# A two-block transformer step on one Trainium2 core: the expert choice with its one-hot product and sum on GpSimd

## The chip, the cores and the metric

The program runs on one core of a Trainium2 chip. The metric is device time in microseconds (us), median of several runs. The engines named below are TensorE (PE in the rows, its weight loads PEld), VectorE (DVE), ScalarE (ACT), GpSimd (POOL) and SyncE (SP), which issues the weight stream.

## What is computed

256 tokens of width 1024 pass through two decoder blocks (retention, dilated attention, two feed-forward parts) and then through two further layers. Each of those ends in a product-key expert stage, which is where the change lies (8 heads, two sides of 128 scores each, `TOPK` = 16):

```python
def peer(xn, wq, k1, k2, u_tab, v_tab):
    q = (xt @ wq).reshape(t, PEER_HEADS, D_KEY)
    q1, q2 = q[..., :D_HALF], q[..., D_HALF:]
    s1 = jnp.einsum("thd,hnd->thn", q1, k1)
    s2 = jnp.einsum("thd,hnd->thn", q2, k2)
    v1, i1 = lax.top_k(s1, TOPK)
    v2, i2 = lax.top_k(s2, TOPK)
    cand = (v1[..., :, None] + v2[..., None, :]).reshape(t, PEER_HEADS, TOPK * TOPK)
    sv, ci = lax.top_k(cand, TOPK)
    e1 = jnp.take_along_axis(i1, ci // TOPK, axis=-1)
    e2 = jnp.take_along_axis(i2, ci % TOPK, axis=-1)
    gates = jax.nn.softmax(sv, axis=-1)
    ...
        hid = jax.nn.gelu(jnp.einsum("td,tkd->tk", xi, u_tab[ei]))
        return jnp.einsum("tk,tkd->td", gi * hid, v_tab[ei])
```

The kernel computes `hid` for all 16384 experts as a dense product and weights it with gates that are zero for the experts not chosen. So the choice of `e1`, `e2` and the gates has to be ready only when that weighting begins.

## The kernel before

All weights come through one stream of tiles of 128 x 1024 floats (512 KB), 878 in all. Each tile goes through the same steps. SyncE loads it into one of four `raw` buffers. ScalarE rounds it to the high half `wh` (`hi`, line 397), into one of two buffers, once TensorE has finished the tile two before (`mm_done`). VectorE writes the low half `wl = raw - wh` (`lo`, line 863) once `w_hi` says that `wh` is there. TensorE waits in `tile_a` (line 1545) for `w_lo` and for the evacuation of its PSUM bank, and then issues 24 matmuls, three passes for each of 8 blocks (lines 1534 to 1536). ScalarE evacuates the result (line 411). So every tile needs one `hi` and one `lo`, in that order, between the end of the tile two before and its own start.

In a layer `k` (0 or 1) of the second pair, 16 tiles give the queries, and 128 more give `hid`. `key_scores` (line 2006) multiplies queries with keys on TensorE, 16 matmuls for two heads, four times per layer, and ScalarE copies the scores to `sc` (line 760).

The expert choice runs on VectorE meanwhile, in 8 rounds `i` per layer (lines 1388 to 1462), each for two heads of one half of the tokens, with 128 tokens on the partitions. Its steps are written between the `lo` calls by hand: `tile()` waits for all the steps so far (`so_far`) and then issues one `lo`, so a round holds exactly 8 of them, and a `lo` is late when the steps ahead of it take long. The steps of a round: copy the scores to `cur` (line 1410); the eight largest of each of four rows of 128 (`max`, 1413), their indices (1416), the row with those struck out (`match_replace`, 1419), the next eight (1422); the 16 x 16 sums `cand` (1425); the indices of the next eight (1428) and their conversion to float `tf` (1430); the same top 16 over two rows of 256 (1432 to 1442); the scores less the largest (`ge`, 1444); the two 4-bit ranks out of each index (1448, 1449) and their conversion (1451). Then for each side `s`: `rank_hot`, a one-hot of the ranks over 16 places, 128x512 in `mh` (1398), and `onto_keys`, its product with the keys `tf` (1404) and the sum over the 16 places (1406) into `ee`. Every counted step raises `pick_step`; 43 of them make a round.

GpSimd issues DMAs alone (lines 330 to 376). In the loop over `k` it loads `bd` and the keys, and goes on to a wait near the end of the kernel.

After the 8 rounds the remaining `lo` follow one another. ScalarE takes the exponentials of `ge` at tile `U_PICK` = 56 of `hid` (line 777), TensorE transposes `ee` and `ge` after tile 59 (line 2034), and the gates are applied from tile 64 on.

Of the kernel before, what the change touches and what calls it, by code (L numbers as in the profile page):

```python
# [20 lines left out]
F32 = mybir.dt.float32  # L21
F32R = mybir.dt.float32r
U32 = mybir.dt.uint32
# [4 lines left out]
P = 128  # L28
# [19 lines left out]
NK, TOPK = 128, 16  # L48
EPS2 = 1e-6
RG_C = 8.0  # L50
PICK_STEPS = 43
MASKED = -1e30
LOWEST = -3.0e38

# [39 lines left out]
def build(nc, stream, x_in, consts, ret_c, att_c, vecs, rg_w, keys, scratch, out):  # L94
    with ExitStack() as ctx:
# [3 lines left out]
        def sem(name):  # L99
            return ctx.enter_context(nc.semaphore(name))  # L100
# [88 lines left out]
        def pick_part(off, *shape):  # L189
# [3 lines left out]
                                                   **dict(zip("abcd", shape)))  # L193


        cur, best = pick_part(1152, 2, 2, P), pick_part(1664, 2, 2, P)
        cand, cand2 = pick_part(1152, 2, 16, 16), pick_part(1664, 2, 256)
        hot = mh[:, 0:2, :].rearrange("p h (a b) -> p h a b", a=16)
        hot_out, hot = hot, hot.bitcast(F32)
        ee, ge = pick_part(0, 2, NC_T * H2, 16), pick_part(512, NC_T * H2, 16)  # L200
        tv, tf, ti = pick_part(768, 2, 2, 16), pick_part(832, 2, 2, 16), pick_part(896, 2, 2, 16).bitcast(U32)
        sv, ci = pick_part(960, 2, 16), pick_part(992, 2, 16).bitcast(U32)
        cr, crf = pick_part(1024, 2, 2, 16).bitcast(U32), pick_part(1088, 2, 2, 16)
        gd = pick_part(2176, 2, NC_T * H2)
        e1T, e2T, gT = (pickT[:, m, :] for m in range(3))

# [37 lines left out]
        k_in, p_s, p_sc, pick_step, p_exp, p_e, p_t, p_tc = (  # L244
            sem(s) for s in "keys_in peer_scores peer_scores_copied peer_pick_step peer_exp "
            "peer_picked peer_turned peer_turned_copied".split())
        g_hot, g_gated = sem("peer_onehots"), sem("peer_gated_rows")
        g_mm, g_mul = sem("peer_gates"), sem("peer_weighted")
        g_put, g_late = sem("peer_gates_put"), sem("peer_late_weighted")
# [79 lines left out]
        @block.gpsimd  # L329
        def _(pool):  # L330
            pool.dma_start(cst[:, :], consts).then_inc(const_in, 16)
            pool.dma_start(vec[:, :], vecs).then_inc(const_in, 16)
            pool.dma_start(xr[:, :, :], x_in.rearrange("(c p) d -> p c d", p=P)).then_inc(x_in_s, 16)
            pool.wait_ge(x_turned, 1)
            pool.dma_start(rc, ret_c).then_inc(retc_in, 16)

            def gains(k):

                pool.dma_start(ln_rows, bass.AP(norm_rows.tensor, 8 * k * P, [[0, P], [32 * P, 2], [1, D]])) \
                    .then_inc(ln_in, 16)  # L340

            pool.wait_ge(rows_copied, 1)
            pool.dma_start(norm_rows, vec_rows[0:104, :]).then_inc(rows_stored, 16)
            pool.wait_ge(rows_stored, 16)
            gains(0)
            pool.wait_ge(n_up, 2)
            gains(1)

            pool.wait_ge(n_lo, split_before[1])
            pool.dma_start(ac[0:33, :], att_c).then_inc(attc_in, 16)  # L350
            pool.wait_ge(b_vecc, G3)
            pool.dma_start(scratch.rearrange("g h x -> h g x"), bv[0:AH, :, :]).then_inc(b_store, 16)
            pool.wait_ge(b_store, 16)
            pool.wait_ge(n_up, 4)
            for h in range(AH):
                if h >= 4:
                    pool.wait_ge(a_b, h - 3)
                pool.dma_start(bs[:, h % 4, :, :], bass.AP(
                    scratch.tensor, h * 384, [[1, P], [AH * 384, G3], [1, T]])).then_inc(b_in[h % 4], 16)

            pool.wait_ge(n_up, 4)
            pool.wait_ge(a_b, AH)
            gains(2)
            pool.wait_ge(n_up, 6)
            gains(3)
            for k in range(2):
                pool.wait_ge(n_lo, split_before[5 + 2 * k])
                pool.dma_start(bd, rg_w[k]).then_inc(bd_in, 16)
                pool.wait_ge(n_lo, split_before[6 + 2 * k])
                pool.dma_start(pk, keys[k]).then_inc(k_in, 16)  # L370
            pool.wait_ge(m_lo, PAIR["b1"] + 10)
            pool.dma_start(ln_rows[:, 0, :], bass.AP(norm_rows.tensor, V_FIN * P, [[0, P], [1, D]])).then_inc(ln_in, 16)
            for c in range(NC_T):
                pool.wait_ge(o_ready, c + 1)
                pool.dma_start(out[c * P:(c + 1) * P, :], o_rows[:, c, :]).then_inc(o_stored, 16)
            pool.wait_ge(o_stored, 32)
# [470 lines left out]
        def _(dve):  # L847
# [364 lines left out]
            for k in range(2):  # L1212
# [175 lines left out]
                for i in range(8):  # L1388
                    pick[0] = 0
                    n = 8 * (i % 2) + 2 * (i // 2)  # L1390

                    def tile():
                        so_far(i)
                        lo(g0 + 29 + at[0] + 2)
                        at[0] += 1

                    def rank_hot(s):
                        count(V.tensor_tensor(hot_out, crf[:, s, :, :].unsqueeze(3).to_broadcast(B4),  # L1398
                                              iota16.unsqueeze(1).unsqueeze(1).to_broadcast(B4), ALU.is_equal))
                        so_far(i)  # L1400

                    def onto_keys(s):

                        count(V.tensor_tensor(hot_out, hot, tf[:, :, s, :].unsqueeze(2).to_broadcast(B4), ALU.mult))  # L1404
                        so_far(i)
                        count(V.tensor_reduce(ee[:, s, n:n + 2, :], hot, AX, ALU.add))  # L1406


                    dve.wait_ge(p_sc, 8 * k + i + 1)
                    count(V.tensor_copy(cur, sc[:, n:n + 2, :, :]))  # L1410
                    tile()
                    for a, s in sides:
                        count(V.max(tv[:, a, s, 0:8], cur[:, a, s, :]))
                    so_far(i)
                    for a, s in sides:
                        count(V.max_index(ti[:, a, s, 0:8], tv[:, a, s, 0:8], cur[:, a, s, :]))
                    tile()
                    for a, s in sides:
                        count(V.match_replace(best[:, a, s, :], tv[:, a, s, 0:8], cur[:, a, s, :], LOWEST))
                    so_far(i)  # L1420
                    for a, s in sides:
                        count(V.max(tv[:, a, s, 8:16], best[:, a, s, :]))

                    tile()
                    count(V.tensor_tensor(cand, tv[:, :, 0, :].unsqueeze(3).to_broadcast(B4),
                                          tv[:, :, 1, :].unsqueeze(2).to_broadcast(B4), ALU.add))
                    for a, s in sides:
                        count(V.max_index(ti[:, a, s, 8:16], tv[:, a, s, 8:16], best[:, a, s, :]))  # L1428
                    so_far(i)
                    count(V.tensor_copy(tf, ti))  # L1430
                    for a in range(2):
                        count(V.max(sv[:, a, 0:8], flat[:, a, :]))
                    tile()
                    for a in range(2):
                        count(V.max_index(ci[:, a, 0:8], sv[:, a, 0:8], flat[:, a, :]))
                        count(V.match_replace(cand2[:, a, :], sv[:, a, 0:8], flat[:, a, :], LOWEST))
                    so_far(i)
                    for a in range(2):
                        count(V.max(sv[:, a, 8:16], cand2[:, a, :]))
                    tile()  # L1440
                    for a in range(2):
                        count(V.max_index(ci[:, a, 8:16], sv[:, a, 8:16], cand2[:, a, :]))

                    count(V.tensor_tensor(ge[:, n:n + 2, :], sv, sv[:, :, 0:1].to_broadcast([P, 2, 16]),
                                          ALU.subtract))

                    tile()
                    count(V.tensor_single_scalar(cr[:, 0, :, :], ci, 4, ALU.logical_shift_right))
                    count(V.tensor_single_scalar(cr[:, 1, :, :], ci, 15, ALU.bitwise_and))
                    so_far(i)  # L1450
                    count(V.tensor_copy(crf, cr))
                    so_far(i)
                    rank_hot(0)
                    so_far(i)
                    onto_keys(0)
                    tile()
                    rank_hot(1)
                    onto_keys(1)
                    so_far(i)
                    assert pick[0] == PICK_STEPS  # L1460
                    lo(g0 + 29 + at[0] + 2)
                    at[0] += 1
# [65 lines left out]
        def _(pe):  # L1528
# [359 lines left out]
            for k in range(2):  # L1888
# [140 lines left out]
                    tile_a(g0 + 45 + j, e0 + 33 + j)  # L2029

                pe.wait_ge(p_e, k + 1)
                for c in range(NC_T):
                    for m, src in enumerate((ee[:, 0, :, :], ee[:, 1, :, :], ge)):
                        ins = nc.tensor.transpose(ps_x[:, c, m * P:(m + 1) * P],
# [170 lines left out]
```

## Time and profile before

| | us |
|---|---|
| median of 3 runs | 2948.59 |
| lowest, highest | 2946.07, 2948.68 |
| the profiled execution | 2945.24 |
| its span, first to last instruction | 2943.5 |
| TensorE busy | 2817.1 (96%) |
| VectorE busy | 1941.7 (66%) |
| ScalarE busy | 1557.4 (53%) |
| GpSimd busy | 23.0 (1%) |
| layer 0: 64 `lo` of the 8 rounds | 1101.1 to 1308.9 |
| layer 1: first and last copy of the scores | 2094.8 to 2276.9 |
| mean granted clock of TensorE | 0.989 |

Busy times of TensorE overlap, since matmuls are pipelined. A start time is therefore a better measure than a duration: steps are read below as the distance from one start to the next on the same engine.

### The profile page before, as it was taken

Reading aid. Unit: us, or ns where it says so; the run is one execution under the profiler, and the core shown is the slowest. Engines: PE = TensorE matmul, PEld = TensorE weight load, DVE = VectorE, ACT = ScalarE, POOL = GpSimd, SP = SyncE. Lnnn points to the kernel's source line nnn. Section 1 sums busy time; section 2 is a strip of 40 time slices with the busy share of each in tenths; the row PEclk is TensorE's granted clock in tenths of the full one; section 3 lists DMA queues with packets and bytes.
Section 4 is the critical chain, followed back from the end, with each engine's and each line's share of the span. In section 5 each row is a group of like instructions: output and inputs, shape, how many; then the busy total and the mean of one; then the engine's idle time right before and its main releaser. Section 6 shows DMA issues by size and latency. Waiting matters only on the chain.

```text
span 2943.5 us, 51574 instructions
## 1 busy us (share of the span) xinstructions
PE 2817.1 (96%) x18787; PEld 2548.3 (87%) x18787; DVE 1941.7 (66%) x3107; ACT 1557.4 (53%) x2815; POOL 23.0 (1%) x38
## 2 busy tenths in 40 slices
PE   8999999999999989999999999998999999999998
PEld 6988987898898879999998888887999999978886
DVE  5656454555555869986886555568799678855555
ACT  4455453555545564446775444456544577644444
POOL 0000000000000000000000000000000000000000
PEclk9999999999999999999999999999999999999999
DMA  6435556664554444454444555543444444455554
GB/s 219 151 130 183 185 170 180 172 159 149 165 184 159 133 130 164 158 170 143 138 144 144 192 190 189 191 161 109 163 161 163 159 140 143 138 178 192 190 189 149
DMA packets 158659, 480.26 MB, mean 163 GB/s; under 512 B 14608, under 2 KB 51472, under 8 KB 158128
## 3 DMA queue, kind: packets, MB, share of 16 engines
q1 hardware_dynamic: 154080, 460.38, 47.4%
q0 software_dynamic: 4432, 17.87, 2.6%
q8 instruction: 98, 1.61, 0.2%
q14 instruction: 49, 0.40, 0.0%
HBM read 477.02 MB, written 1.18 MB: 162 GB/s over the span
## 4 chain that ended last, share of the span: by engine, by line
PE 77%; DVE 16%; ACT 4%; issue 2%; DMA 1%; POOL 0%; DVEq 0%; ACTq 0%; POOLq 0%
PE ps L1534 23%; PE ps L1536 23%; PE ps L1535 23%; DVE wl L863 6%; PE ps L2049 4%; ACT wh L397 2%; DVE arena L1251 1%; DVE mh L1404 1%; DVE picks L1406 1%; DVE mh L1398 1%; PE ps L1653 1%; DMA raw<-stream_dram 1%; DVE xr L882 0%; PE ps L2015 0%; DVE picks L1428 0%
## 5 line engine op out<-in xcount | busy, mean ns | idle before, releaser
L863 DVE TENSOR_TENSOR wl<-raw,wh 128x1024 fp32r<-128x1024 f32 x878 | 1075.5, 1225 | 889.6 <-ACT wh L397 883.6
L397 ACT ACTIVATE wh<-raw 128x1024 fp32r<-128x1024 f32 x878 | 929.9, 1059 | 1281.8 <-PE ps L1536 1270.9
L1534 PE MATMUL ps<-xh,wh 128*128 128x256 f32 x3920 | 1138.9, 291 | 24.4 <-DVE wl L863 22.9
L1535 PE MATMUL ps<-xl,wh 128*128 128x256 f32 x3920 | 1111.5, 284 | 0.0
L1536 PE MATMUL ps<-xh,wl 128*128 128x256 f32 x3920 | 1110.9, 283 | 0.0
L1534 PEld LDWEIGHTS ps<-xh,wh 128*128 128x128 f32 x3920 | 753.4, 192 | 49.2 <-issue 36.9
L1535 PEld LDWEIGHTS ps<-xl,wh 128*128 128x128 f32 x3920 | 754.6, 193 | 0.4
L1536 PEld LDWEIGHTS ps<-xh,wl 128*128 128x128 f32 x3920 | 753.7, 192 | 0.0
L1534 PE MATMUL ps<-wh,mh 128*128 128x512 f32 x1304 | 516.6, 396 | 13.7 <-DVE ml L875 8.8
L1536 PE MATMUL ps<-wh,ml 128*128 128x512 f32 x1304 | 512.1, 393 | 0.0
L1535 PE MATMUL ps<-wl,mh 128*128 128x512 f32 x1304 | 511.0, 392 | 0.0
L1534 PEld LDWEIGHTS ps<-wh,mh 128*128 128x128 f32 x1304 | 246.0, 189 | 90.9 <-issue 33.3
L1536 PEld LDWEIGHTS ps<-wh,ml 128*128 128x128 f32 x1304 | 246.0, 189 | 54.2
L1535 PEld LDWEIGHTS ps<-wl,mh 128*128 128x128 f32 x1304 | 246.7, 189 | 43.5
L411 ACT ACTIVATE arena<-ps 128x256 f32<-128x256 f32 (+1 forms) x360 | 132.2, 367 | 0.2
L1534 PE MATMUL ps<-wh,xh 128*128 128x512 f32 x248 | 101.4, 409 | 15.5 <-DVE wl L863 5.7
L875 DVE TENSOR_TENSOR ml<-arena,mh 128x512 fp32r<-128x512 f32 x158 | 108.1, 686 | 4.4 <-ACT mh L443 4.4
L443 ACT ACTIVATE mh<-arena 128x512 fp32r (+1 forms) x158 | 96.9, 615 | 7.1 <-DVE arena L1494 3.9
L1494 DVE TENSOR_TENSOR arena<-arena,ps 128x260 f32<-128x260 f32 (+42 forms) x128 | 71.1, 556 | 42.7 <-ACT arena L817 40.9
L1535 PE MATMUL ps<-wl,xh 128*128 128x512 f32 x248 | 98.8, 398 | 0.0
L1536 PE MATMUL ps<-wh,xl 128*128 128x512 f32 x248 | 98.4, 397 | 0.0
L797 ACT ACTIVATE picks<-mh,pickT 128x128 f32<-128x128 f32 x256 | 81.5, 398 | 4.4 <-DVE mh L1482 4.4
(280 smaller groups left out, 2040.1 us busy)
## 6 DMA issues: line engine op xcount, KB each, us to landing
raw<-stream_dram SPq DMA_DIRECT2D x878, 512.0 KB, 3.3
arena<-bias_scratch POOLq DMA_DIRECT2D x16, 384.0 KB, 9.8
arena<-norm_rows POOLq DMA_DIRECT2D x4, 1024.0 KB, 6.8
arena<-keys_dram POOLq DMA_DIRECT2D x2, 1024.0 KB, 5.1
arena<-ret_c_dram POOLq DMA_DIRECT2D x1, 1344.0 KB, 6.1
xr<-x_dram POOLq DMA_DIRECT2D x1, 1024.0 KB, 9.2
out_dram<-arena POOLq DMA_DIRECT2D x2, 512.0 KB, 2.9
arena<-rg_w_dram POOLq DMA_DIRECT2D x2, 256.0 KB, 2.9
```

The costliest lines, as they stand in the source:

```text
L397: A(wh[b % 2][:, :, :], raw[:, b % 4, :].rearrange("p (a b) -> p a b", a=DB), ACT.Copy) \
L411: A(dst, src, func, scale=scale, **kw).then_inc(evac, 1)
L443: A(mh[:, s:s + 2, :], src, ACT.Copy).then_inc(m_hi, 1)
L797: ins = A(gated[n % 3][:, j, :], oh[n % 2][:, j, :].bitcast(F32), ACT.Copy, scale=gT[:, t:t + 1])
L863: V.tensor_tensor(wl[b % 2][:, :, :], raw[:, b % 4, :].rearrange("p (a b) -> p a b", a=DB), wh[b % 2][:, :, :].bitcast(F32), ALU.subtract) ...
L875: V.tensor_tensor(ml[:, s:s + 2, :], src, mh[:, s:s + 2, :].bitcast(F32), ALU.subtract) \
L1251: ins = V.scalar_tensor_tensor(out=cy[:, b, :], in0=src, scalar=vec[:, w:w + 1], in1=cy[:, b, :], op0=ALU.mult, op1=ALU.add)
L1494: V.tensor_tensor(h, h, ps_a[:, n % 4, :].rearrange("p (t m) -> p m t", t=4)[:, 0:known, :], ALU.mult).then_inc(g_mul, 1)
L1534: M(out_ap, lh, rh, start=first, stop=False, skip_group_check=skip)
L1535: M(out_ap, lh, rl, start=False, stop=False, skip_group_check=skip)
L1536: return M(out_ap, ll, rh, start=False, stop=last, skip_group_check=skip)
L2049: ins = M(ps_a[:, n % 4, j * P:(j + 1) * P], gated[n % 3][:, j, :], oh[n % 2][:, 4 + j, :].bitcast(F32), start=True, stop=True)
```

## The change

The copy of the scores is left out; `cur` is a view of `sc`. VectorE keeps everything up to the two one-hots. Those go to two buffers (`mh` for side 0, `ml` for side 1), each raises a semaphore `p_rank`, and GpSimd does the rest: the product with the keys, and the sum over 16 places as four additions that halve the number of places (8, 4, 2, then the last into `ee`), five instructions for a side, ten for a round, each waiting for the one before. `tf` has two buffers, in `pickT`. VectorE waits for GpSimd's `p_ee` ahead of a one-hot (round before, same side) and ahead of `tf` (two rounds before); TensorE waits for it ahead of the transposes. The steps are also dealt out anew between the 8 `lo` of a round, and `PICK_STEPS` is 36.

```diff
--- before.py
+++ after.py
@@ -48,7 +48,7 @@
 NK, TOPK = 128, 16
 EPS2 = 1e-6
 RG_C = 8.0
-PICK_STEPS = 43
+PICK_STEPS = 36
 MASKED = -1e30
 LOWEST = -3.0e38
 
@@ -193,14 +193,16 @@
                                                    **dict(zip("abcd", shape)))
 
 
-        cur, best = pick_part(1152, 2, 2, P), pick_part(1664, 2, 2, P)
+        best = pick_part(1664, 2, 2, P)
         cand, cand2 = pick_part(1152, 2, 16, 16), pick_part(1664, 2, 256)
-        hot = mh[:, 0:2, :].rearrange("p h (a b) -> p h a b", a=16)
-        hot_out, hot = hot, hot.bitcast(F32)
+        hot_out = [t[:, 0:2, :].rearrange("p h (a b) -> p h a b", a=16) for t in (mh, ml)]
+        hot = [t.bitcast(F32) for t in hot_out]
+        tf = [pickT[:, 0, 64 * n:64 * n + 64].rearrange("p (a b c) -> p a b c", a=2, b=2) for n in range(2)]
+        crf = pickT[:, 0, 128:192].rearrange("p (a b c) -> p a b c", a=2, b=2)
         ee, ge = pick_part(0, 2, NC_T * H2, 16), pick_part(512, NC_T * H2, 16)
-        tv, tf, ti = pick_part(768, 2, 2, 16), pick_part(832, 2, 2, 16), pick_part(896, 2, 2, 16).bitcast(U32)
+        tv, ti = pick_part(768, 2, 2, 16), pick_part(896, 2, 2, 16).bitcast(U32)
         sv, ci = pick_part(960, 2, 16), pick_part(992, 2, 16).bitcast(U32)
-        cr, crf = pick_part(1024, 2, 2, 16).bitcast(U32), pick_part(1088, 2, 2, 16)
+        cr = pick_part(1024, 2, 2, 16).bitcast(U32)
         gd = pick_part(2176, 2, NC_T * H2)
         e1T, e2T, gT = (pickT[:, m, :] for m in range(3))
 
@@ -244,6 +246,7 @@
         k_in, p_s, p_sc, pick_step, p_exp, p_e, p_t, p_tc = (
             sem(s) for s in "keys_in peer_scores peer_scores_copied peer_pick_step peer_exp "
             "peer_picked peer_turned peer_turned_copied".split())
+        p_rank, p_hot, p_ee = sem("peer_ranks"), sem("peer_keys_at_ranks"), sem("peer_keys_summed")
         g_hot, g_gated = sem("peer_onehots"), sem("peer_gated_rows")
         g_mm, g_mul = sem("peer_gates"), sem("peer_weighted")
         g_put, g_late = sem("peer_gates_put"), sem("peer_late_weighted")
@@ -368,6 +371,21 @@
                 pool.dma_start(bd, rg_w[k]).then_inc(bd_in, 16)
                 pool.wait_ge(n_lo, split_before[6 + 2 * k])
                 pool.dma_start(pk, keys[k]).then_inc(k_in, 16)
+                B4 = [P, 2, 16, 16]
+                for i in range(8):
+                    n = 8 * (i % 2) + 2 * (i // 2)
+                    for s in range(2):
+                        done = 2 * (8 * k + i) + s
+                        pool.wait_ge(p_rank, done + 1)
+                        nc.gpsimd.tensor_tensor(hot_out[s], hot[s], tf[i % 2][:, :, s, :].unsqueeze(2).to_broadcast(B4),
+                                                ALU.mult).then_inc(p_hot, 1)
+                        for step, w in enumerate((8, 4, 2)):
+                            pool.wait_ge(p_hot, 4 * done + step + 1)
+                            nc.gpsimd.tensor_tensor(hot_out[s][:, :, :, 0:w], hot[s][:, :, :, 0:w],
+                                                    hot[s][:, :, :, w:2 * w], ALU.add).then_inc(p_hot, 1)
+                        pool.wait_ge(p_hot, 4 * done + 4)
+                        nc.gpsimd.tensor_tensor(ee[:, s, n:n + 2, :].unsqueeze(3), hot[s][:, :, :, 0:1],
+                                                hot[s][:, :, :, 1:2], ALU.add).then_inc(p_ee, 1)
             pool.wait_ge(m_lo, PAIR["b1"] + 10)
             pool.dma_start(ln_rows[:, 0, :], bass.AP(norm_rows.tensor, V_FIN * P, [[0, P], [1, D]])).then_inc(ln_in, 16)
             for c in range(NC_T):
@@ -1394,45 +1412,37 @@
                         lo(g0 + 29 + at[0] + 2)
                         at[0] += 1
 
-                    def rank_hot(s):
-                        count(V.tensor_tensor(hot_out, crf[:, s, :, :].unsqueeze(3).to_broadcast(B4),
-                                              iota16.unsqueeze(1).unsqueeze(1).to_broadcast(B4), ALU.is_equal))
-                        so_far(i)
-
-                    def onto_keys(s):
-
-                        count(V.tensor_tensor(hot_out, hot, tf[:, :, s, :].unsqueeze(2).to_broadcast(B4), ALU.mult))
-                        so_far(i)
-                        count(V.tensor_reduce(ee[:, s, n:n + 2, :], hot, AX, ALU.add))
-
-
                     dve.wait_ge(p_sc, 8 * k + i + 1)
-                    count(V.tensor_copy(cur, sc[:, n:n + 2, :, :]))
-                    tile()
+                    cur = sc[:, n:n + 2, :, :]
                     for a, s in sides:
                         count(V.max(tv[:, a, s, 0:8], cur[:, a, s, :]))
-                    so_far(i)
+                    tile()
                     for a, s in sides:
                         count(V.max_index(ti[:, a, s, 0:8], tv[:, a, s, 0:8], cur[:, a, s, :]))
                     tile()
                     for a, s in sides:
                         count(V.match_replace(best[:, a, s, :], tv[:, a, s, 0:8], cur[:, a, s, :], LOWEST))
-                    so_far(i)
+                    tile()
                     for a, s in sides:
                         count(V.max(tv[:, a, s, 8:16], best[:, a, s, :]))
-
-                    tile()
+                    so_far(i)
                     count(V.tensor_tensor(cand, tv[:, :, 0, :].unsqueeze(3).to_broadcast(B4),
                                           tv[:, :, 1, :].unsqueeze(2).to_broadcast(B4), ALU.add))
+                    tile()
                     for a, s in sides:
                         count(V.max_index(ti[:, a, s, 8:16], tv[:, a, s, 8:16], best[:, a, s, :]))
                     so_far(i)
-                    count(V.tensor_copy(tf, ti))
+                    if 8 * k + i >= 2:
+                        dve.wait_ge(p_ee, 2 * (8 * k + i - 1))
+                    count(V.tensor_copy(tf[i % 2], ti))
+                    tile()
                     for a in range(2):
                         count(V.max(sv[:, a, 0:8], flat[:, a, :]))
+                    so_far(i)
+                    for a in range(2):
+                        count(V.max_index(ci[:, a, 0:8], sv[:, a, 0:8], flat[:, a, :]))
                     tile()
                     for a in range(2):
-                        count(V.max_index(ci[:, a, 0:8], sv[:, a, 0:8], flat[:, a, :]))
                         count(V.match_replace(cand2[:, a, :], sv[:, a, 0:8], flat[:, a, :], LOWEST))
                     so_far(i)
                     for a in range(2):
@@ -1440,23 +1450,21 @@
                     tile()
                     for a in range(2):
                         count(V.max_index(ci[:, a, 8:16], sv[:, a, 8:16], cand2[:, a, :]))
-
                     count(V.tensor_tensor(ge[:, n:n + 2, :], sv, sv[:, :, 0:1].to_broadcast([P, 2, 16]),
                                           ALU.subtract))
-
-                    tile()
+                    so_far(i)
                     count(V.tensor_single_scalar(cr[:, 0, :, :], ci, 4, ALU.logical_shift_right))
                     count(V.tensor_single_scalar(cr[:, 1, :, :], ci, 15, ALU.bitwise_and))
                     so_far(i)
                     count(V.tensor_copy(crf, cr))
                     so_far(i)
-                    rank_hot(0)
-                    so_far(i)
-                    onto_keys(0)
-                    tile()
-                    rank_hot(1)
-                    onto_keys(1)
-                    so_far(i)
+                    for s in range(2):
+                        if 8 * k + i:
+                            dve.wait_ge(p_ee, 2 * (8 * k + i - 1) + s + 1)
+                        V.tensor_tensor(hot_out[s], crf[:, s, :, :].unsqueeze(3).to_broadcast(B4),
+                                        iota16.unsqueeze(1).unsqueeze(1).to_broadcast(B4),
+                                        ALU.is_equal).then_inc(p_rank, 1)
+                    dve.wait_ge(p_rank, 2 * (8 * k + i) + 2)
                     assert pick[0] == PICK_STEPS
                     lo(g0 + 29 + at[0] + 2)
                     at[0] += 1
@@ -2029,6 +2037,7 @@
                     tile_a(g0 + 45 + j, e0 + 33 + j)
 
                 pe.wait_ge(p_e, k + 1)
+                pe.wait_ge(p_ee, 16 * (k + 1))
                 for c in range(NC_T):
                     for m, src in enumerate((ee[:, 0, :, :], ee[:, 1, :, :], ge)):
                         ins = nc.tensor.transpose(ps_x[:, c, m * P:(m + 1) * P],
```

## Rows read from the trace of the kernel before

**Rows 1.** The page's part on busy time: each engine's us, share and instructions.

```profile
PE 2817.1 (96%) x18787; PEld 2548.3 (87%) x18787; DVE 1941.7 (66%) x3107; ACT 1557.4 (53%) x2815; POOL 23.0 (1%) x38
```

**Rows 2.** Waits, 1153.6 to 1307.8 us: waiter, releaser, us in total, times, longest.

```profile
PEld ps L1534 <- issue: 14.4, 30, 0.9
PE ps L1534 <- DVE wl L863: 8.2, 18, 0.7
```

**Rows 3.** Busy time by stretch: window, its length, PE, PEld, DVE, ACT, POOL, clock, DMA.

```profile
1320.00:1340.00 20.00, 19.81 (x167) 19.64 (x166) 9.65 (x11) 10.81 (x17) 0.00 (x0) 1.00 0.54 184
...
1101.11:1308.92 207.81, 198.35 (x1591) 191.83 (x1590) 193.16 (x553) 90.96 (x149) 0.00 (x0) 1.00 0.49 160
```

**Rows 4.** Timeline behind the last round, all engines: start, duration, engine, line, [idle before].

```profile
1308.92 1.23 DVE L863 TENSOR_TENSOR wl<-raw,wh 128x1024 fp32r<-128x1024 f32 x1
1310.27 0.38 PE L1534 MATMUL ps<-xh,wh 128*128 128x256 f32 x1 [0.18 <-DVE wl L863]
1313.44 1.06 ACT L397 ACTIVATE wh<-raw 128x1024 fp32r<-128x1024 f32 x1 [1.98 <-PE ps L1536]
1314.53 1.23 DVE L863 TENSOR_TENSOR wl<-raw,wh 128x1024 fp32r<-128x1024 f32 x1 [2.09 <-ACT wh L397]
```

**Rows 5.** Timeline of VectorE over one round, of layer 0.

```profile
1155.87 0.42 DVE L1410 COPY picks<-arena 128x512 f32<-128x512 f32 x1
1157.11 1.23 DVE L863 TENSOR_TENSOR wl<-raw,wh 128x1024 fp32r<-128x1024 f32 x1 [0.82 <-ACT wh L397]
1158.25 0.87 DVE L1413 MAX8 picks<-picks 128x8 f32<-128x128 f32 x4
1159.15 0.09 DVE L1416 MATCH_VALUE_LOAD picks<-picks 128x8 f32 x1
...
1160.41 1.23 DVE L863 TENSOR_TENSOR wl<-raw,wh 128x1024 fp32r<-128x1024 f32 x1
...
1162.72 0.87 DVE L1422 MAX8 picks<-picks 128x8 f32<-128x128 f32 x4
1163.62 1.23 DVE L863 TENSOR_TENSOR wl<-raw,wh 128x1024 fp32r<-128x1024 f32 x1
...
1165.37 0.08 DVE L1428 MATCH_VALUE_LOAD picks<-picks 128x8 f32 x1
...
1166.54 0.20 DVE L1430 CAST picks<-picks 128x64 f32<-128x64 uint32 x1
...
1167.43 1.22 DVE L863 TENSOR_TENSOR wl<-raw,wh 128x1024 fp32r<-128x1024 f32 x1
...
1170.27 0.76 DVE L1439 MAX8 picks<-picks 128x8 f32<-128x256 f32 x2
1171.06 1.23 DVE L863 TENSOR_TENSOR wl<-raw,wh 128x1024 fp32r<-128x1024 f32 x1
...
1173.21 1.23 DVE L863 TENSOR_TENSOR wl<-raw,wh 128x1024 fp32r<-128x1024 f32 x1
...
1174.65 0.19 DVE L1451 CAST picks<-picks 128x64 f32<-128x64 uint32 x1
1174.87 0.69 DVE L1398 TENSOR_TENSOR mh<-picks,cst 128x512 fp32r<-128x512 f32 x1
1175.67 0.69 DVE L1404 TENSOR_TENSOR mh<-mh,picks 128x512 fp32r<-128x512 f32 x1
1176.40 0.69 DVE L1406 TENSOR_REDUCE picks<-mh 128x32 f32<-128x512 f32 x1
1177.12 1.22 DVE L863 TENSOR_TENSOR wl<-raw,wh 128x1024 fp32r<-128x1024 f32 x1
...
1181.57 0.42 DVE L1410 COPY picks<-arena 128x512 f32<-128x512 f32 x1
```

**Rows 6.** Timeline of TensorE: the keys' scores, and the transposes of the choice.

```profile
1108.40 1.95 PE L2015 MATMUL ps<-arena 128*128 128x128 f32 x16
...
1325.19 0.82 PE L2034 MATMUL ps<-cst,picks 128*128 128x128 f32 x6
```

## Prediction

> **What bounds the kernel now.** I read the page's busy times first: TensorE at 96% against VectorE's 66% says that on the whole VectorE has room, and GpSimd computes nothing [rows 1]. An average hides stages, so the waits of the stretch with the rounds of layer 0 come next. There TensorE stands for VectorE's `lo` 18 times, 8.2 us, and its weight loads for another 14.4 us [rows 2]. Then the stretches: 64 tiles of the rounds take 207.81 us [rows 3]. Free of the rounds TensorE issues 167 matmuls in 20 us [rows 3], 0.120 each, so 24 of them make a tile of 2.88 us. 64 tiles are 184.3, and three groups of key scores at 1.95 [rows 6] bring it to 190.2. So the stage loses 17.6 us, in both layers some 35: the most that anything done to VectorE's rounds can bring.
>
> How a `lo` that comes late costs time is read from four starts behind a round [rows 4]. TensorE begins a tile 1.35 us after its `lo` began (1308.92 to 1310.27). The `hi` that waits for the end of that tile starts 3.17 after the tile did (1310.27 to 1313.44), and the next `lo` can start 1.09 after it (to 1314.53). 3.17 + 1.09 + 1.35 is 5.61, against 5.76 for two tiles. So a `lo` may be 0.15 late, no more, and whatever is beyond that stops TensorE. Only the `lo` right after such a stop has as much slack more as the stop lasted.
>
> From start to start a `lo` holds VectorE for 1.14 (1157.11 to 1158.25) [rows 5]. So 1.74 us of steps fit between two `lo` at TensorE's pace. The gaps between the eight `lo` of the round shown are 3.30, 3.21, 3.81, 3.63, 2.15, 3.91, about 3.30 and 2.39 [rows 5]: the steps hold 0.42 to 2.77 us. Following all `lo`, `hi` and tiles through these rules gives 25.62 us a round; copy to copy it is 25.70 [rows 5]. The rules hold, and I use them on the new order.
>
> **The change part by part.** The copy of 0.42 goes [rows 5]; what reads `sc` in its place reads the same number of elements in SBUF, cost nothing more. The two products and two sums go: from 1175.67 to 1177.12 they are 1.45 a side, 2.90 a round. The remaining steps are new between the `lo`, each priced by start-to-start distances [rows 5]:
> 1. four `max`: 1159.15 - 1158.25 = 0.90.
> 2. four `max_index`: 1160.41 - 1159.15 = 1.26.
> 3. four `match_replace`: 1162.72 - 1160.41 - 1.14 = 1.17.
> 4. four `max` and the sums `cand`: 0.90 + (1165.37 - 1163.62 - 1.14 = 0.61, with a wait 0.71) = 1.61.
> 5. four indices and the cast: 1.17 + 0.23 = 1.40.
> 6. two `max` over 256, two indices: 0.79 + 0.89 = 1.68 (the indices are the 1.01 from behind the `lo` of 1171.06 to 1173.21, less the small subtraction).
> 7. two `match_replace` and two `max`: 0.91 + 0.79 = 1.70 (1170.27 - 1167.43 - 1.14 = 1.70 holds two replaces and two indices; 0.79 is for the indices).
> 8. two indices and `ge` 1.01; two rank instructions 1174.65 - 1173.21 - 1.14 = 0.30; cast 0.22; two one-hots, the first 0.60 to the second's start (0.61 for `cand`, of the same shape, before an instruction that does not wait), the second 0.72 with its wait. Together 2.85.
>
> Seven of eight fit into 1.74. The eighth is 1.11 too long; less the 0.15 of slack it stops TensorE for 0.96. A round becomes 8 x 2.88 + 0.96 = 24.00, against 25.70. In rounds 0 and 1 TensorE has the key scores as well, so VectorE's surplus cost less before: there the same rules give a gain of 1.0 for the two. Rounds 2 to 7 gain 6 x 1.62 (25.62 against 24.00) = 9.7. One layer 10.7, both 21.4 us. That is the sum if GpSimd's work is free.
>
> The new waits of VectorE for `p_ee` are free. Ahead of `tf` it waits for a round two back, ahead of a one-hot for one back, about 23 us earlier. GpSimd's ten instructions a round would cost 6.9 us at 0.69 each, VectorE's time for the largest of them [rows 5], and 21 at three times that: they fit in 24. Behind a waiting one-hot there would be a `lo`, so this is where a very slow GpSimd would show. At the end of the stage the transposes begin at 1325.2 [rows 6], 16 us after the last `lo` of the rounds [rows 4], room enough for the last two sides (6.9). The stream's queue and GpSimd's DMAs aren't passed: the two loads of a layer are issued ahead of the loop, and those of layer 1 are wanted 700 us later. Steps that read `crf` and `tf` in `pickT`, and a second buffer in `ml`, cost the same as before, whichever tile they lie in.
>
> What has no row is what GpSimd's instructions do to VectorE, since it never computes beside it here [rows 1]. Call `c` what the last `lo` of a round loses, the one on the path: the product of side 0 becomes ready while the second one-hot runs, and the `lo` follows at once. From below `c` is 0: an added engine takes nothing from the others' work, so a gain is excluded. From above: the product stands in front of the `lo` for its whole length. The nearest row for that length is VectorE's own 0.69 for the same 128x512 product [rows 5]; twice that, 1.38, is my upper end for an engine without a row. I take 0.69, the middle of 0 and 1.38 and the nearest row. Each 0.1 of `c` costs 0.1 in every round, 1.4 us in all. With 0.69 a round is 24.69, a layer gains 6 x 0.93 + 0.3 = 5.8, both 11.7. The first `lo` of the next round meets the rest of GpSimd's chain too, but has 1.0 to 1.7 of slack from the stop; the second may lose a little, which is inside the range.
>
> The Trainium skill speaks against this change: SBUF — State Buffer, section Who interferes with whom, says that a VectorE instruction with two SBUF inputs (as `lo` is) contends with a GpSimd instruction that reads SBUF, and that the one that comes second stands until the first is done. GPSIMD Engine Reference, section Performance versus the Vector engine, gives 4497 ns for an addition of 2048 columns; a quarter, 1.12 us, is an estimate for the product here. By the two, `c` is 1.12 and the sum a gain of about 5 us. No row here can show either.
>
> **The rivals.**
> (a) GpSimd's work is free, `c` = 0: gain 21.4, 2927 us. For it: each `lo` shown takes 1.22 or 1.23, whatever ScalarE and TensorE do beside it [rows 4, 5], so engines do work side by side here. Against: both engines would read the same memory at the same moments.
> (b) The product stands fully in front of the `lo` and is nearly twice VectorE's time, `c` about 1.0 to 1.8: 2941 to 2954, about 2947 at 1.38, no change that can be measured.
> (c) Slower: GpSimd holds up more than one `lo` in a round. The first point of loss is `c` = 1.46, where the two layers come out even; every further `lo` that is caught pays in full, since from the second on it has 0.15 of slack. With `c` = 1.4 and 0.6 at the second or third `lo`, a round is 26.0, 0.3 over now, and rounds 0 and 1 lose more: about 2957. It decides from a GpSimd chain so long that side 1's product, too, falls on a `lo`: above 3 us a side, so at 0.6 for each of the five.
> (d) The change doesn't do what it says: GpSimd needs over 23 us a round, and the one-hots wait for it. Each instruction would have to take 2.3 us, three times the 0.69; under 2 in 100, and it would be far slower than now.
>
> **How the numbers follow.** The profiled execution was 2945.24, 3.35 below the median; I work from the median. 2948.59 - 11.7 = 2936.9. Chances: forecast (`c` 0.3 to 1.0) 0.38, (a) 0.24, (b) 0.25, (c) with (d) 0.13. The range goes from 2926 (case a with a little more) to 2953 (most of b). A measurement can tell 0.2%, 5.9 us, from no change: faster is the forecast, (a), and the edge of (b), 0.66; within is the rest of (b), 0.21; slower 0.13.
>
> **What would show it.** Eight `lo` per round with seven gaps near 2.88 and one of 4.0 + `c`; a round of 24.0 + `c`; TensorE waiting for the `lo` once a round only. The `lo` behind the second one-hot is the place to read `c`, by its duration or by the distance to it. Wrong: `lo` instructions of more than 1.23 in several places, a `max` or index step longer than now, or a gap ahead of a one-hot. The rest of the kernel, 2528 us outside the two stages, shouldn't move.

## The result and the profile after

The changed kernel takes 2953.41 us (median of 20 runs, 2950.36 to 2958.55), the kernel before 2947.60 in the same comparison. The ratio is 1.0021, with a 95% interval of 1.0014 to 1.0028: 5.8 us slower, where 11.7 us faster was forecast, and past the bound of 2953. The profiled execution has a span of 2952.2 us, against 2943.5.

The page of after, busy times, to be set beside [rows 1]:

```profile
PE 2820.4 (96%) x18787; PEld 2561.1 (87%) x18787; DVE 1911.8 (65%) x3027; ACT 1556.6 (53%) x2815; POOL 158.2 (5%) x198
```

VectorE did lose 30 us of work and 80 instructions. The loss must lie in how the rounds run. In after `lo` is line 881, GpSimd's product line 380 and its first three additions line 384. The stretches of after (window, length, PE, PEld, DVE, ACT, POOL, clock, DMA):

```profile
1178.00:1203.00 25.00, 23.23 (x191) 22.85 (x190) 22.08 (x63) 10.48 (x19) 8.94 (x10) 1.00 0.49 168
1228.00:1253.00 25.00, 23.23 (x182) 23.03 (x181) 20.85 (x62) 9.49 (x16) 8.05 (x10) 0.93 0.48 161
1310.00:1320.00 10.00, 8.23 (x56) 8.03 (x56) 4.99 (x3) 2.84 (x5) 7.38 (x10) 0.83 0.33 111
```

In the rounds of before the granted clock was 1.00 throughout, as in [rows 3]. Now some stretches have 1.00 and some 0.93, and the one right behind the last round 0.83. From `lo` to `lo` behind the one-hots the rounds of layer 0 last 25.1, 25.3, 26.6, 26.6, 25.1 and 26.6 us, those of layer 1 26.5, 26.5, 25.1, 26.5, 26.5 and 25.1; all were 25.70 before. So there are two sorts of round, one 0.6 shorter than before and one 0.9 longer.

The timeline of after at the end of one round, with one line of a later round, VectorE and GpSimd together, in order of start (start, duration, engine, line):

```profile
1153.98 0.69 DVE L1464 TENSOR_TENSOR ml<-pickT,cst 128x512 fp32r<-128x512 f32 x1
1154.14 1.66 POOL L380 TENSOR_TENSOR mh<-mh,pickT 128x512 fp32r<-128x512 f32 x1 [17.23 <-DVE mh L1464]
1154.70 2.19 DVE L881 TENSOR_TENSOR wl<-raw,wh 128x1024 fp32r<-128x1024 f32 x1
1155.88 3.36 POOL L384 TENSOR_TENSOR mh<-mh 128x256 fp32r<-128x256 f32 x3
...
1157.70 1.38 DVE L881 TENSOR_TENSOR wl<-raw,wh 128x1024 fp32r<-128x1024 f32 x1
...
1159.51 1.29 POOL L380 TENSOR_TENSOR ml<-ml,pickT 128x512 fp32r<-128x512 f32 x1
1160.88 2.51 POOL L384 TENSOR_TENSOR ml<-ml 128x256 fp32r<-128x256 f32 x3
1161.34 1.35 DVE L881 TENSOR_TENSOR wl<-raw,wh 128x1024 fp32r<-128x1024 f32 x1 [1.21 <-ACT wh L415]
...
1237.86 1.63 POOL L384 TENSOR_TENSOR ml<-ml 128x256 fp32r<-128x256 f32 x3
```

The `lo` that starts at 1154.70 takes 2.19 us where it took 1.23 [rows 5]. GpSimd's product ends at 1155.80 and the `lo` 1.09 later, at 1156.89: it did next to nothing until the product was over. The hold goes both ways. The same product alone, beside searches with one input, takes 1.29 (1159.51), but 1.66 where it meets the second one-hot. The three additions take 1.63 where no `lo` meets them (1237.86), 2.51 where one does (side 1) and 3.36 where two do (side 0). The next `lo`, 1.38, loses 0.15 to the addition of 128 columns, and the third, 1.35, loses 0.12 to side 1's. So `c`, which the prediction reads at the last `lo` alone, is 0.96, not 0.69, and VectorE and GpSimd do hold each other up whole instructions at a time. With it the Trainium skill's rule holds here (SBUF — State Buffer, Who interferes with whom: the second to issue stands until the first is done). The estimate of 1.12 us for the product, worked out from the figure in the Trainium skill's GPSIMD Engine Reference (Performance versus the Vector engine), was nearer to the 1.29 than the 0.69 that I took. The prediction had named `lo` of more than 1.23 in several places as a sign that it is wrong, and here are three in a round.

What follows on TensorE and ScalarE in the round at 1231.7 us:

```profile
1234.02 0.38 PE L1542 MATMUL ps<-xh,wh 128*128 128x256 f32 x1 [1.77 <-DVE wl L881]
```

```profile
1238.68 1.06 ACT L415 ACTIVATE wh<-raw 128x1024 fp32r<-128x1024 f32 x1 [5.07 <-PE ps L1544]
```

TensorE stands for 1.77 us, once a round, where before it stood up to 0.7 at a time in several places [rows 2]. The tile that begins at 1234.02 is over 4.66 us later (the `hi` that waits for its end starts at 1238.68), where 3.17 was the rule [rows 4]: 1.49 us more. In the stretch beside it:

```profile
1235.00:1240.00 5.00, 5.00 (x31) 5.00 (x31) 2.29 (x10) 1.32 (x3) 4.35 (x7) 0.66 0.64 210
```

TensorE is busy all the time, and only 31 matmuls start in 5 us where 42 did at 0.120 each [rows 3]. Its granted clock is 0.66 on average there, that is partly 1.2 and partly 2.4 GHz. This is what the prediction had no term for. In the two stages of this profile the granted clock is 0.50 in nine such stretches, each beginning within 1.3 us of the end of one of the 14 stops of 1.8 us: four in layer 0, five in layer 1. Seven lie in the rounds and make them the long ones, one lies behind the last round of each layer.

### The profile page after: what moved, and what is told of

It reads as the page before. It is cut to its first block, busy times and chain, and to the rows that moved or that the text cites. A ratio compares the mean times of both kernels' runs of the same rounds, so it can differ in the third digit from the quotient of the medians.

```text
span 2952.2 us, 51671 instructions
## 1 busy us (share of the span) xinstructions
PE 2820.4 (96%) x18787; PEld 2561.1 (87%) x18787; DVE 1911.8 (65%) x3027; ACT 1556.6 (53%) x2815; POOL 158.2 (5%) x198
## 4 chain that ended last, share of the span: by engine, by line
PE 81%; DVE 12%; ACT 4%; issue 2%; DMA 1%; DVEq 0%; POOL 0%; ACTq 0%; POOLq 0%
PE ps L1542 25%; PE ps L1544 24%; PE ps L1543 24%; DVE wl L881 5%; PE ps L2058 4%; ACT wh L415 2%; DVE arena L1269 1%; PE ps L1661 1%; DMA raw<-stream_dram 1%; DVE xr L900 0%; PE ps L2023 0%; DVE picks L1443 0%; PE ps L1797 0%; DVE picks L1446 0%; DVE picks L1452 0%
## 5 line engine op out<-in xcount | busy, mean ns | idle before, releaser
L881 DVE TENSOR_TENSOR wl<-raw,wh 128x1024 fp32r<-128x1024 f32 x878 | 1093.3, 1245 | 930.1 <-ACT wh L415 924.8
```

The source lines that it names most:

```text
L881: V.tensor_tensor(wl[b % 2][:, :, :], raw[:, b % 4, :].rearrange("p (a b) -> p a b", a=DB), wh[b % 2][:, :, :].bitcast(F32), ALU.subtract) ...
```

## The experiments

Three theories stood against each other. S: GpSimd's product lengthens the one stop of a round, and a stop of that length brings TensorE's clock down. G: GpSimd's activity brings the clock down. T: every single stop does. What is left out of the computation is said in each expectation.

**GpSimd's product and first additions left out.**

```diff
-                        nc.gpsimd.tensor_tensor(hot_out[s], hot[s], tf[i % 2][:, :, s, :].unsqueeze(2).to_broadcast(B4),
-                                                ALU.mult).then_inc(p_hot, 1)
-                        for step, w in enumerate((8, 4, 2)):
-                            pool.wait_ge(p_hot, 4 * done + step + 1)
-                            nc.gpsimd.tensor_tensor(hot_out[s][:, :, :, 0:w], hot[s][:, :, :, 0:w],
-                                                    hot[s][:, :, :, w:2 * w], ALU.add).then_inc(p_hot, 1)
-                        pool.wait_ge(p_hot, 4 * done + 4)
```

> The changed kernel without GpSimd's product and its first three additions, so the keys are not chosen; only the last addition of 32 columns runs. Theory S (GpSimd's product holds the memory port in front of the low half behind the one-hots, which lengthens TensorE's one stop of a round from about 1.0 to 1.9 us, and after a stop of that length TensorE's granted clock falls to half for some us): every low half 1.23 us, a stop of 1.0 a round, 24.0 us a round, no stretch of the rounds at half clock, about 21 us under the kernel before (2926 to 2930). Theory G (GpSimd's own activity lowers the clock, the stop only adds its length): the same 2926 to 2930, since GpSimd is nearly idle. Theory T (any stop in one piece, 1.0 us too, lowers the clock): rounds of 24.0 and 25.5 in turn, about 2937.

Measured: 2928.42 us, ratio 0.9924 (0.9907 to 0.9941), 20.3 under the kernel before. The rounds are 24.1 us. T falls: a stop of 0.8 us each round leaves the clock at 1.00. Who waited for whom from 1150 to 1300 us (waiter, releaser, us in total, times, longest), and the clock of the same stretch:

```profile
PE ps L1535 <- DVE wl L874: 4.9, 6, 0.8
```

```profile
1150.00:1300.00 150.00, 145.10 (x1197) 143.72 (x1195) 131.97 (x398) 67.24 (x112) 12.18 (x14) 1.00 0.53 175
```

This is also the forecast's sum without the unknown: 24.00 a round and 21.4 us were worked out for `c` = 0.

**The stop without GpSimd.** To the run above, three searches were added in front of the last `lo`:

```diff
+                    for m in range(3):
+                        count(V.max(pickT[:, 2, 8 * m:8 * m + 8], flat[:, 0, :]))
+                    so_far(i)
                     dve.wait_ge(p_rank, 2 * (8 * k + i) + 2)
```

> As the run without GpSimd's product and additions, and three more searches for a maximum over 256 columns (about 1.1 us) on VectorE in front of the last low half of each round. The stop of TensorE is again some 2 us long, with no GpSimd beside it. Theory S: rounds of 25.1 and 26.6 us mixed as in the changed kernel, stretches at half clock after the stops, total within 3 us of the changed kernel (about 2950 to 2956). Theory G: all rounds 25.1 us, clock 1.00 through the rounds, about 6 us under the kernel before (2942).

Measured: 2953.60 us, ratio 1.0015 (1.0005 to 1.0025), the time of the changed kernel. The rounds are 25.0, 25.1, 26.6, 26.6, 25.1, 26.6. Waits and stretches of this run:

```profile
PE ps L1538 <- DVE wl L874: 10.8, 6, 1.8
```

```profile
1150.00:1300.00 150.00, 139.19 (x1113) 138.01 (x1112) 128.54 (x391) 62.20 (x103) 5.05 (x12) 0.97 0.49 162
1236.00:1240.00 4.00, 4.00 (x23) 4.00 (x22) 2.05 (x9) 0.60 (x1) 0.00 (x0) 0.58 0.81 259
```

The same stops (1.8 us, six of them, 10.8 in total; the changed kernel has 10.6), the same two sorts of round, the same clock (0.97 from 1150 to 1300 in both), with GpSimd idle around the fall (0.00 in the second stretch). Half clock follows 6 of the 14 stops of this profile. G falls.

**One and two searches in place of three.**

> As the run with three added searches, with one. The search adds 0.34 us or a little more to the stop of a round: about 1.2 us idle instead of the 0.8 of the run without and the 1.8 of the run with three. Theory S (the length of the one stop is what brings the clock down): rounds of about 24.4 us with few or no stretches at half clock; 13 to 18 us under the kernel before. If every added 0.1 us only adds itself, the same 14 to 16.

> The same with two searches: the stop about 1.5 us idle. By its length alone rounds of 24.7 us, 9 to 12 us under the kernel before. With half-clock stretches after some of the stops (theory S, the clock falls somewhere between stops of 0.8 and 1.8) up to 15 us more, so from 10 under to 4 over it. Which of the two it is tells between which stops the fall sets in.

Measured: 2930.99 us with one (0.9944, 0.9927 to 0.9961) and 2936.48 with two (0.9961, 0.9947 to 0.9975). The rounds are 24.43 and 24.76, the longest stop 1.1 and 1.5, and the clock is 1.00 from 1150 to 1300 in both. The stretch of the run with two:

```profile
1150.00:1300.00 150.00, 141.15 (x1166) 139.96 (x1165) 132.39 (x401) 66.04 (x110) 5.04 (x12) 1.00 0.51 169
```

In a row, each set against the kernel before of its own comparison: no search -20.3 us, one -16.6, two -11.2, three +4.9. The first two steps cost 3.7 and 5.5 us, about 16 rounds by 0.33; the third costs 16.1. In neither profile does half clock follow any of the 14 stops of its rounds, so the fall sets in between stops of 1.5 and 1.8 us in these rounds.

**The product of side 0 held back until the `lo` is written.**

```diff
                         pool.wait_ge(p_rank, done + 1)
+                        if s == 0:
+                            pool.wait_ge(w_lo, START[f"b{k}"] + 45 + 8 * i)
```

> The changed kernel with one more wait: GpSimd starts the product of side 0 only when the low half behind the one-hots is written. All of GpSimd's work stays. Theory S: that low half takes 1.23 us, the next one or two are held up by 0.3 to 0.6 us, which the slack after the stop takes up; rounds of 24.0 to 24.4, no half clock, 15 to 20 us under the kernel before. Theory G: the same rounds with half-clock stretches, 5 to 9 us under it.

Measured: 2937.82 us, ratio 0.9966 (0.9952 to 0.998), 10.9 under the kernel before, where 15 to 20 were expected; nothing is left out of what is computed. Its clock from 1150 to 1300 is 1.00. But the rounds are 25.0 us, not 24.0 to 24.4. Its timeline, VectorE's `lo` and GpSimd's product of side 1:

```profile
1202.56 1.70 DVE L883 TENSOR_TENSOR wl<-raw,wh 128x1024 fp32r<-128x1024 f32 x1
1206.20 2.20 DVE L883 TENSOR_TENSOR wl<-raw,wh 128x1024 fp32r<-128x1024 f32 x1 [0.89 <-ACT wh L417]
```

```profile
1206.03 1.29 POOL L382 TENSOR_TENSOR ml<-ml,pickT 128x512 fp32r<-128x512 f32 x1
```

The product of side 0 (from 1201.88) now meets the next `lo` (1.70), behind which TensorE doesn't stop, and so shifts the chain that side 1's product meets the third (2.20). I had left that second collision out. It makes a stop of its own, and it leaves a round of the same length as the changed kernel's good ones, 25.0 against 25.1, but in two stops of at most 0.8:

```profile
PE ps L1544 <- DVE wl L883: 8.8, 12, 0.8
```

8.8 us of standing in twelve pieces leaves the clock at 1.00; 10.6 in six pieces does not. Between the two kernels lie 16.7 us (10.9 under and 5.8 over the kernel before), of which the standing, 1.8 us in this stretch and about as much in the other layer, explains about 4; the nine stretches at half clock, at 1.45 to 1.49 us each, are some 13.

**Everything on VectorE, in the new order.** The copy is out, the one-hots, products and sums come one round later and lie between the other steps; GpSimd computes nothing.

```diff
+                    if i:
+                        rank_hot(i - 1, 0)
                     for a, s in sides:
                         count(V.max(tv[:, a, s, 0:8], cur[:, a, s, :]))
                     tile()
...
+                    if i:
+                        product(i - 1, 0)
                     tile()
...
+                    if i:
+                        key_sum(i - 1, 0)
+                    if i:
+                        rank_hot(i - 1, 1)
                     tile()
```

`product(i - 1, 1)` stands ahead of the cast of `tf`, `key_sum(i - 1, 1)` behind the last indices.

> The copy of the scores left out and the steps dealt out anew between the low halves, with one-hots, products and sums all on VectorE and one round later; GpSimd computes nothing. It tells how much of the change is the new order. VectorE's steps of a round add up to 24.5 us at 1.14 for each low half, so with short stops spread over the round: rounds of 24.5 to 24.9, clock 1.00, 10 to 14 us under the kernel before by both theories. If so, GpSimd's share of the change was a loss.

Measured: 2924.07 us, ratio 0.9911 (0.9894 to 0.9927), 24.7 under the kernel before, where 10 to 14 were expected. The rounds are 24.07, below the expected 24.5: steps that no longer wait for the one just ahead start some 0.1 us earlier (the search behind a one-hot starts 0.60 after it, not 0.72). From 1140 to 1290 the clock is 1.00.

So an even order, with the one-hots taken out of the long piece, is worth 25 us with nothing moved to another engine. The change differs from it in two things at once, the long piece that it leaves and GpSimd's product behind it, and lost 5.8.

**GpSimd's work without the long piece, with and without holding it back.** One-hots one round later, at two places; in the first of the two runs the products also wait for a `lo`:

```diff
+GATE = (0, 5)
...
+                        if i < 7:
+                            pool.wait_ge(w_lo, START[f"b{k}"] + 46 + 8 * i + GATE[s])
```

> All of GpSimd's work as in the changed kernel, but the one-hots come one round later, side 0 ahead of the first search for maxima and side 1 behind the match_replace, and each product waits for a low half (side 0 for the first, side 1 for the sixth of that round), so that it runs beside steps of VectorE with one input. Theory S: the longest piece of VectorE between two low halves is 1.8 us, the products (1.28 alone) fit into pieces of 1.26 and 1.70 with 0.1 to 0.3 left over on the next low half; rounds of 23.1 to 23.7 us, clock 1.00, 25 to 35 us under the kernel before. If GpSimd's additions (0.73, 0.46, 0.30, 0.24) hold low halves up too, 24.0 to 24.5 and 15 to 20 us under it.

> The same without the waits of the products for a low half: GpSimd starts each as soon as it can. The one long piece of the round (2.85 us) is gone, the collisions stay. Theory S: no stop over 1.2 us, so no half clock; collisions of 0.5 to 1.0 us for each of the two products, part of them in slack: rounds of 23.8 to 24.7, 12 to 22 us under the kernel before. The distance to the run with the waits is the price of the collisions.

Measured: 2922.37 us with the waits (0.9913, 0.9897 to 0.993) and 2925.85 without (0.9922, 0.9906 to 0.9939). The rounds are 23.80 and 24.23, clock 1.00 from 1140 to 1290 in both; the distance, 0.43 a round, is the price of the collisions, though the intervals of the two times overlap. The gain with the waits is 24.6 us where 25 to 35 were expected, without them 21.1 where 12 to 22 were. The 23.80 misses the expected 23.1 to 23.7 by a little, since the additions still catch a `lo` twice a round. Timeline of the run with the waits, GpSimd:

```profile
1205.56 2.50 POOL L387 TENSOR_TENSOR mh<-mh 128x256 fp32r<-128x256 f32 x3
```

and VectorE at the same place:

```profile
1205.69 1.69 DVE L884 TENSOR_TENSOR wl<-raw,wh 128x1024 fp32r<-128x1024 f32 x1 [0.60 <-ACT wh L418]
```

The product (1.31 us from 1204.18) fits beside the searches, and the first addition (0.73) starts 0.13 ahead of the `lo` and costs it 0.46.

**Only the sums on GpSimd.** The kernel with everything on VectorE, but `key_sum` replaced by GpSimd's four additions behind each product.

> The order of the kernel with everything on VectorE, but the two sums of a round go to GpSimd as four additions each, the products stay on VectorE. Only 3.5 us of GpSimd's work a round is left, its longest instruction 0.73. VectorE's steps add up to less than TensorE's 23.04. Theory S: rounds of 23.1 to 23.8, clock 1.00; 25 to 33 us under the kernel before, a little under the one with all on VectorE (24.09 a round, 24.7 under). If collisions with the 0.73 us addition eat what is moved, equal to it within 3 us.

Measured: 2923.77 us, ratio 0.9916 (0.9899 to 0.9932), 23.2 under the kernel before, where 25 to 33 were expected; rounds of 23.77. Within the intervals it is level with the kernel with everything on VectorE: the 0.3 us a round (some 4 us in all) that the sums free is not seen in the medians, and this profile has one stretch at half clock behind the rounds of each layer that the other doesn't have.

**The copy alone.**

```diff
-                    count(V.tensor_copy(cur, sc[:, n:n + 2, :, :]))
+                    cur = sc[:, n:n + 2, :, :]
                     tile()
```

> The kernel before with the copy of the scores left out and nothing else changed. The copy stands in the one piece of a round behind which VectorE waits for the high half anyway (0.82 us of waiting), so the wait should grow by 0.42 and the round stay at 25.7 us: within 3 us of the kernel before. If the copy were on the path it would be 0.42 x 16, 6.7 us less.

Measured: 2947.32 against 2947.63, ratio 1.0 (0.999 to 1.0009), rounds of 25.70 as before. Nothing, as expected.

## Why the prediction was wrong

- **What bounds the stage, and the rules of a late `lo`: right.** They gave 24.00 for a round without collisions and 21.4 us in all; 24.1 and 20.3 were measured. With the measured `c` of 0.96 they give 24.96 a round; the good rounds take 25.1, 1.0 more than those without GpSimd's work.
- **The price of each step on VectorE: right** for seven pieces of 0.90 to 1.70; the last `lo` comes 4.00 after the one ahead of it (1227.69 to 1231.69) where 2.85 + 1.14 = 3.99 was worked out. That the copy costs nothing by itself is shown too.
- **`p_ee`, the transposes, the DMAs: right.** No engine waits for GpSimd in the rounds.
- **`c`: under-sized.** I priced GpSimd's product by VectorE's 0.69; it takes 1.29 by itself, and 0.96 of it falls on the `lo`. At the prediction's 1.4 us for each 0.1 of `c` that leaves a gain of 8.0 us in place of 11.7. This is a term of the wrong size, and the smaller part of the miss: 0.96 lies inside the forecast's own 0.3 to 1.0.
- **The step that failed** is the sentence that each 0.1 of `c` costs 0.1 a round, 1.4 us in all, and with it case (b), 2941 to 2954 for `c` up to 1.8. The runs with added searches show it true for stops up to 1.5 us. At 1.8 TensorE goes on at half clock for a while and the tile behind the stop takes 1.5 us more, after 9 of the 14 stops of the changed kernel. The stop at the end of the layer is followed by such a stretch too (0.83 from 1310 to 1320): from the last `lo` of the rounds to the first one-hots of the gates it is 33.4 us now, where it was 30.9, and 0.96 of that is the length of that `lo`. Two terms together: 8.0 us gained by the rules, and nine stretches at 1.45 to 1.49, some 13 lost to the clock, give about 5 lost; 5.8 was measured. The jump of 16 us between two and three searches, of which 5 are the search, puts the clock's price at about 11 us where half clock follows six stops; six at 1.49 are 9, and the intervals of the two times, 3 and 4 us either way, allow both.
- **Case (c), the slower one, had the right sign and the wrong mechanism.** It wanted more than one `lo` caught in a round. There were three (0.96, 0.15 and 0.12), but TensorE stops only once in a round, so the second and third fell into slack. What made it slower was that the standing came in one piece. I read the sum of the stops and not the longest one: in the rounds of before TensorE stood for 8.2 us in pieces of at most 0.7 [rows 2], and the clock was 1.00. The trace of before could have warned, behind the rounds of layer 0:

```profile
1342.49 1.19 PE L2049 MATMUL ps<-mh,picks 128*128 128x128 f32 x8 [2.10 <-ACT picks L797]
```

```profile
1343.60:1346.80 3.20, 3.20 (x17) 3.20 (x17) 2.61 (x3) 1.49 (x6) 0.00 (x0) 0.50 0.30 95
```

A stop of 2.10 us, and TensorE at half clock 1.1 us after its end. The same stop in layer 1, up to 2335.03, is followed by a clock of 1.00 up to 2345.

- **Small slips in the sums.** At 1.4 us for each 0.1 the two kernels come out even at `c` = 1.53, not 1.46, and `c` = 1.8 gives 2952, not 2954. Neither decides anything.
- **The rest of the kernel** was to stay as it is. Set side by side by the starts of the same `lo`, the profiled execution of after lost 1.2 us in layer 0, from the rounds to behind the first one-hots of the gates, and 5.3 in layer 1; the other 2.3 of its 8.8 lie outside, where stretches at half clock fall in other places in the two profiles.

Left open: why the fall follows some stops of 1.8 us and not others (after 9 of 14 in the changed kernel, 6 of 14 with three searches and GpSimd's work left out). No run here varied what lies between the stops.

## What to carry to other kernels

Where an engine feeds TensorE too slowly, spread the shortage: here stops of up to 1.5 us cost about their length, and one of 1.8 us cost 1.5 us more whenever half clock followed it; so price the longest stop of an order, not only its sum. Before work is moved to GpSimd to relieve VectorE, deal the same steps out evenly on VectorE: here that alone gave 25 us, and the best place tried for GpSimd's work gave no more that could be measured. If it is moved, let its instructions start behind a two-input instruction of VectorE and run beside steps with one input, because a `lo` that came second here stood for the rest of GpSimd's instruction.

## What the runs showed of the hardware

- A GpSimd product of 128x512 with two inputs takes 1.29 us, additions of 256, 128, 64 and 32 columns 0.73, 0.46, 0.30 and 0.24, with nothing of VectorE's two-input work beside them. The product is 1.9 times VectorE's 0.69, the smallest addition still 0.24.
- The hold is by whole instructions and in both directions: the `lo` of 1.23 became 2.19 behind a product, and GpSimd's addition of 256 columns took 1.58 in place of 0.73 where it came second to a `lo`. The searches on VectorE (one input) beside GpSimd kept their durations: four `max` 0.86 against 0.87 before, and the product beside index searches took 1.29.
- TensorE's granted clock stayed at 2.4 GHz through rounds with one stop of 0.8, 1.1 or 1.5 us, and went to 1.2 GHz for a stretch after 9 of 14 stops of 1.8 us with GpSimd at work and 6 of 14 without. Between two stops of the rounds TensorE had been busy for over 20 us each time.
